# GpSimd takes seven low-weight subtractions of the long convolution's layer, and two output panels of the short convolutions run side by side

## The reference, cut to what matters

```python
def short_conv_mixer(h, w_in, conv_w, w_out):
    b_gate, c_gate, u = jnp.split(h @ w_in, 3, axis=-1)
    return (b_gate * depthwise_conv3(c_gate * u, conv_w)) @ w_out

def hyena_mixer(h, w_in, short_w, short_b, f_w1, ..., w_out):
    v, x1, x2 = jnp.split(depthwise_conv3(h @ w_in, short_w, short_b), 3, axis=-1)
    h_freq = hyena_filters(...)      # decayed filters, divided by their sum, in frequency
    z = x1 * long_conv(v, 0)
    z = x2 * long_conv(z, 1)
    return z @ w_out
```

## Time and profile before

| | |
|---|---|
| median of three runs | 1741.15 us (1740.19 to 1745.28) |
| profiled execution, its own time | 1742.05 us |
| its span | 1740.2 us |
| TensorE, VectorE, ScalarE, GpSimd busy | 97%, 71%, 56%, 1% |
| mean granted TensorE clock | 0.99 of full speed |
| phase `in2` and its filters | about 603 to 712 us |

### The profile page before, as it was taken

The page is one execution under the profiler, slowest core; times in us unless marked ns, Lnnn a source line. Parts: engine busy times, 40 slices in busy tenths (PEclk is TensorE's granted clock), DMA queues, the critical chain, the costliest instruction groups (busy, mean ns, idle before and its releaser), DMA issues.

```text
span 1740.2 us, 37287 instructions
## 1 busy us (share of the span) xinstructions
PE 1686.8 (97%) x13776; PEld 1594.9 (92%) x13776; DVE 1229.4 (71%) x2013; ACT 970.9 (56%) x1352; POOL 13.0 (1%) x20
## 2 busy tenths in 40 slices
PE   7999999999999999999999999999999999999997
PEld 7999999888999987569999999999999876799997
DVE  6887766587776687888776688776666665587764
ACT  4477744365775444206775446775455645477742
POOL 0000200000000000000000000000000000000000
PEclk9999999999999998999999999999999999999999
DMA  6577665433867554205666556667554432166662
GB/s 214 163 215 236 193 227 154 146 110 116 246 201 226 161 158 135 70 1 166 197 195 218 161 175 187 203 192 251 163 173 146 137 142 61 61 185 199 191 226 68
DMA packets 79547, 290.17 MB, mean 167 GB/s; under 512 B 9739, under 2 KB 12140, under 8 KB 79340
## 3 DMA queue, kind: packets, MB, share of 16 engines
q1 hardware_dynamic: 79468, 289.11, 53.1%
HBM read 288.03 MB, written 1.05 MB: 166 GB/s over the span
## 4 chain that ended last, share of the span: by engine, by line
PE 87%; DVE 9%; issue 2%; ACT 2%; DVEq 0%; DMA 0%; SPq 0%; ACTq 0%
PE bank L581 24%; PE bank L583 24%; PE bank L582 24%; DVE wlo L1553 2%; PE bank L869 2%; PE bank L856 1%; PE bank L810 1%; DVE conv_cv L1669 1%; PE bank L600 1%; PE bank L601 1%; PE bank L602 1%; PE bank L985 1%; DVE hy_z L1810 1%; PE bank L1081 1%; PE bank L1091 1%
## 5 line engine op out<-in xcount | busy, mean ns | idle before, releaser
L1185 ACT CAST whi<-raw 128x1024 fp32r<-128x1024 f32 (+1 forms) x490 | 539.2, 1102 | 330.0 <-PE bank L583 300.1
L581 PE MATMUL bank<-xq_h,whi 128*128 128x256 f32 x2384 | 664.1, 279 | 3.7 <-DVE wlo L1553 3.4
L583 PE MATMUL bank<-xq_l,whi 128*128 128x256 f32 x2384 | 657.7, 276 | 0.0
L582 PE MATMUL bank<-xq_h,wlo 128*128 128x256 f32 x2384 | 657.7, 276 | 0.0
L1553 DVE TENSOR_TENSOR wlo<-raw,whi 128x1024 fp32r<-128x1024 f32 (+1 forms) x491 | 629.9, 1283 | 6.3 <-ACT whi L1185 3.6
L581 PEld LDWEIGHTS bank<-xq_h,whi 128*128 128x128 f32 x2384 | 448.2, 188 | 14.1 <-issue 8.1
L582 PEld LDWEIGHTS bank<-xq_h,wlo 128*128 128x128 f32 x2384 | 448.1, 188 | 1.7 <-issue 1.7
L583 PEld LDWEIGHTS bank<-xq_l,whi 128*128 128x128 f32 x2384 | 448.0, 188 | 0.0
L583 PE MATMUL bank<-ffn_hl,whi 128*128 128x256 f32 x880 | 242.5, 276 | 0.0
L582 PE MATMUL bank<-ffn_hh,wlo 128*128 128x256 f32 x880 | 242.5, 276 | 0.0
L581 PE MATMUL bank<-ffn_hh,whi 128*128 128x256 f32 x880 | 242.4, 275 | 0.0
(11 more groups left out here) (342 smaller groups left out, 2379.7 us busy)
## 6 DMA issues: line engine op xcount, KB each, us to landing
raw<-in_w SPq DMA_DIRECT2D x414, 512.0 KB, 3.6
raw<-in_w SPq DMA_DIRECT2D x80, 704.0 KB, 4.1
att_bias<-in_bias SPq DMA_DIRECT2D x4, 512.0 KB, 5.5
hy_w<-in_filt_w SPq DMA_DIRECT2D x8, 256.0 KB, 5.5
hy_decay<-in_decay SPq DMA_DIRECT2D x4, 512.0 KB, 4.6
mla_uq<-in_uq SPq DMA_DIRECT2D x1, 1152.0 KB, 5.3
x<-in_xT SPq DMA_DIRECT2D x1, 1024.0 KB, 5.8
out<-x SPq DMA_DIRECT2D x8, 128.0 KB, 2.0
```

The costliest lines, as they stand in the source:

```text
L581: pe.matmul(ps, whi[:, slot, wc], hi[:, k, cols], start=first, stop=False)
L582: pe.matmul(ps, wlo[:, slot, wc], hi[:, k, cols], start=False, stop=False)
L583: mm = pe.matmul(ps, whi[:, slot, wc], lo[:, k, cols], start=False, stop=last)
L1185: nc.scalar.copy(slices(whi, p % RING, k, to), raw_slices(p % RING, k, to)).then_inc(panel_hi, 1)
```

## The change

GpSimd gets seven subtractions of phase `in2`: at steps 5, 8, 11, 14, 16, 19 and 22 VectorE leaves out `split_lo`. GpSimd waits for ScalarE's cast of that panel and subtracts. VectorE, after its two taps of the same step, waits for GpSimd's count and writes one element of a small tile, which raises `panel_lo` in its place, so that this semaphore is still raised by one engine and in order.

`merged` becomes `paired` with the phase's name, rows and semaphore as arguments. It is now called also for `out0` and `out3`, in place of `product`: two panels side by side over the eight slices, then six in turn.

```diff
+GPSIMD_SPLITS = (5, 8, 11, 14, 16, 19, 22)
-    eps = sb("eps", [P, 2])
+    eps = sb("eps", [P, 3])
+    gpsimd_lo = sem("gpsimd_lo")
...
-        def merged():
-
-            ph = PH["w_o"]
+        def paired(name, hi, lo, ready):
+
+            ph = PH[name]
             for j in range(2):
                 pe.wait_ge(panel_lo, ph.p0 + j + 1)
                 pe.wait_ge(bank_free, ph.t0 + j + 1)
             for k in range(K8):
-                pe.wait_ge(y_lo, YBASE["mrg"] + k + 1)
+                pe.wait_ge(ready[0], ready[1] + k + 1)
                 for j in range(2):
...
             for j in range(2, 8):
-                panel(ph, j // 4, j % 4, mg["yh2"], mg["yl2"], Q, None)
+                panel(ph, j // 4, j % 4, hi, lo, Q, None)
...
             if kind == "conv":
-                product(f"out{layer}", bufs["yh"], bufs["yl"], Q, (y_lo, YBASE[f"in{layer}"]))
+                paired(f"out{layer}", bufs["yh"], bufs["yl"], (y_lo, YBASE[f"in{layer}"]))
...
         mask_bias()
+        for step in GPSIMD_SPLITS:
+            p = PH["in2"].p0 + step + 3
+            pool.wait_ge(panel_hi, p + 1)
+            nc.gpsimd.tensor_tensor(wlo[:, p % RING, 0:K8 * P], raw[:, p % RING, 0:K8 * P],
+                                    whi[:, p % RING, 0:K8 * P].bitcast(F32), ALU.subtract).then_inc(gpsimd_lo, 1)
...
-                split_lo(ph, 0, i, j, k)
+                if i * 4 + j not in GPSIMD_SPLITS:
+                    split_lo(ph, 0, i, j, k)
 
                 dve.wait_ge(first_tap, TAPS["in2"] + j + 1 + 4 * i)
                 for t in (1, 2):
...
+                if i * 4 + j in GPSIMD_SPLITS:
+                    dve.wait_ge(gpsimd_lo, GPSIMD_SPLITS.index(i * 4 + j) + 1)
+                    V.memset(eps[0:1, 2:3], 0.0).then_inc(panel_lo, 1)
```

More of the change, by code:

```diff
@@ L920, in merged @@
                     wc = slice(k * P, (k + 1) * P)
-                    pe.matmul(ps, whi[:, slot, wc], mg["yh2"][:, k, Q], start=k == 0, stop=False)
-                    pe.matmul(ps, wlo[:, slot, wc], mg["yh2"][:, k, Q], start=False, stop=False)
-                    mm = pe.matmul(ps, whi[:, slot, wc], mg["yl2"][:, k, Q], start=False, stop=k == K8 - 1)
+                    pe.matmul(ps, whi[:, slot, wc], hi[:, k, Q], start=k == 0, stop=False)
+                    pe.matmul(ps, wlo[:, slot, wc], hi[:, k, Q], start=False, stop=False)
+                    mm = pe.matmul(ps, whi[:, slot, wc], lo[:, k, Q], start=False, stop=k == K8 - 1)
                     if k == K8 - 1:
@@ L1131, in _ @@
         product("mla_out", ml["yh"], ml["yl"], Q, None)
-        merged()
+        paired("w_o", mg["yh2"], mg["yl2"], (y_lo, YBASE["mrg"]))
         product("up4", *xs[norm], (x_lo, C * norm), norm)
```

## The result

The changed kernel takes 1749.65 us in the median of eight runs (1748.53 to 1751.46), the kernel before 1741.11 us in eight; the ratio is 1.0052, with an interval of 1.0043 to 1.0061. It is slower by 7.5 to 10.6 us. The forecast was 1749.1.

A forecast was written before the change was run, and what follows sets the result against it. TensorE bounds the kernel, busy 97%, with about 9 us of waits winnable. Holds 7.8, memsets +0.4, step 5 -0.3, side-by-side panels -0.2 make +8.0 us on 1741.15: 1749.1, range 1739.5 to 1752.0.

The forecast's parts named there:

- likeliest case: Long convolution's input product: GpSimd's reading holds VectorE's two-input operations; 1749.1 us, own range 1746.0 to 1752.0, chance 0.57.
- added elements: VectorE's seven added waits and one-element memsets, 0.1 us each; 0.4 us on the path at steps 5, 11, 14 and 19.
- second part: First two short-convolution output panels side by side: layer 3 trades a 0.67 us wait for 0.44, net -0.2; layer 0 nothing.
- The floor: VectorE's taps in the input product need ScalarE's first tap, so removing seven subtractions wins only 0.3 us of path.
- GpSimd's duration: Each 128x1024 subtraction on GpSimd taken as 2.4 us, between estimates of 2.2 and 2.7.
- The direction of the hold: A reading GpSimd operation was assumed to hold VectorE's two-input operations for its whole duration; the trace showed only GpSimd held.
- Step 5's hold: VectorE's subtraction due at 621.60 starts 1.7 us late behind GpSimd; taps and decayed filter come 1.25 us later.
- step 8's: VectorE's maximum of L1829, which TensorE waits for, is held until GpSimd stops reading at 635.6: +1.6 us.
- step 16's: VectorE's taps due at 669.29 wait for GpSimd until 671.15, straight before the maximum TensorE needs: +1.85 us.
- A: Rival: VectorE is not held, as GpSimd yields or both run; -0.1 us, 1741.0 us; chance 0.30.
- B: Rival: VectorE always wins and GpSimd is late, twice or so on the path; +1 us, 1742 us; chance 0.07.
- C: Rival: ScalarE's tap is not the floor, and TensorE's waits at L801 and L823 shrink; up to -6 us, 1735; chance 0.06.

The follow-up runs named there:

- experiment 3: The change without side-by-side output panels, its seven subtractions left out on both engines, VectorE's waits and one-element writes kept; 1739.0 us, ratio 0.9995.
- Experiment 8: Kernel before, with ScalarE's first tap put ahead of its cast in the long convolution's input product; 1738.32 us beside 1741.09, ratio 0.9984.
- experiment 5: The change without side-by-side output panels, with a GpSimd memset of the low weights in place of each subtraction; 1740.94 us in one run.
- experiment 6: The change without side-by-side output panels, with a one-input GpSimd copy in place of each subtraction; 1740.02 us in one run.
- experiment 7: Kernel before, with two subtractions (steps 6 and 15) moved to GpSimd, started just before VectorE's decayed-filter products; 1741.34 us in one run.
- experiment 10: Kernel before, with ScalarE's first tap ahead of its cast and seven subtractions left out on both engines, VectorE writing one element; 1738.08 us in one run.
- experiment 2: The changed kernel with no subtraction on GpSimd, only the first two output panels side by side; 1739.90 us beside 1740.45, ratio 1.0001.

## Why the prediction was right

Measured +8.5 us in the medians, forecast +8.0, in the middle of the likeliest case's own range. The mechanism is the one forecast. That the number came so near is in part luck: for the stretch the sum had 7.8 us of holds and 0.4 of added elements, and TensorE's waits there rose by 7.2, so with the 0.2 of the second part the waits account for 7.0 of the 8.5. The rest is not in TensorE's waits. In the profiled runs, 8.2 us apart, 0.8 of it is the clock and the start of the program, and 0.4 is left; in the others it is open.

- **What bounds the kernel.** That only about 9 us of TensorE's waits can be won there, and that the subtractions are on none of the long ones, held: experiment 3 took them away and changed the waits by 0.1.
- **The floor.** ScalarE's tap after the cast was named as what the taps wait for. After the change seven pairs of taps wait for it, idle 0.67 us each. Experiment 8 put it ahead of the cast, and the waits fell by 1.5 us.
- **GpSimd's duration.** Taken as 2.4, between 2.2 and 2.7 from three rows; measured 2.34 alone. The estimate from VectorE's ratio (2.2) was nearer than that from GpSimd's memset (2.7).
- **The direction of the hold.** This was the main assumption: the trace of before showed a held GpSimd and no held VectorE. The seven long operations and experiments 5, 6 and 7 show it, for GpSimd operations that read SBUF and VectorE operations with two SBUF inputs. The rule of the Trainium skill (SBUF — State Buffer, "Who interferes with whom") says this; the trace agrees, with 3.00 us for 1.22, and with nothing held beside a memset (1216 ns).
- **The prices.** Step 5's hold was put at 1.7 and is 1.78; step 8's at 1.6 and is 1.49; step 16's at 1.85 and is 1.68. By place of TensorE's waits: before the filter sums +5.2, and 0.3 more for late low weights, where steps 5, 8, 14 and 16 summed to 5.8; `wing_weights` +0.7 for 0.75; the first turn +0.5 for 0.8; the second turn +0.5 for 0.45. Sum 7.2 for 7.8. That low weights would once be late (0.3 us, behind step 5) was not foreseen.
- **The added elements.** 0.06 us each as taken from the earlier trace rows; the 0.4 charged to the path looks too much, since experiment 3 shows 0.1 less waiting with relief and writes together, where 0.3 won and 0.4 lost had been forecast.
- **The second part.** -0.2 by the exchange of 0.67 for 0.48, which the rows show and the times can't.
- **The rivals.** A is wrong on the hold. What it would have given stands in experiments 3 and 5: waits of 9.7 and 9.8 us for 9.8, and a ratio of 0.9995 in experiment 3. B falls, as VectorE lost 12.5 us. C falls with experiment 3; with the tap first it would have held for 1.1 us (experiment 10).

## What to carry to other kernels

An elementwise operation given to GpSimd is no relief of VectorE if it reads SBUF while VectorE has two-input operations to do: it took 2.34 us where VectorE had spent 1.13, and each one held VectorE for 1.5 to 2.05. Beside products with one input in PSUM it held nothing, and TensorE's waits rose by 0.2 us. A hold doesn't show as idle or as a wait of VectorE, only as an operation that takes longer than its like, so look there. And before an engine is relieved, look at what its next operation waits for; here it was the order of two operations on another engine.

## What the hardware showed that I had not expected

TensorE's granted clock in one and the same stretch was 0.91 of full speed in one kernel's run and 0.95 in another's with the same code there and the same waits (before and experiment 2), which is 2.6 us of length, more than most of these edits are worth. In before's trace it is half speed (1.2 GHz) for a time that begins 1.3 us after the first of the two waits before the filter sums has ended (635.3 us), and for another that begins within the second (668.7 to 672.3 us); in the rest of the stretch it is full speed (2.4 GHz). Window, length, busy time and count as above, then the granted clock:

```profile
636.70:643.30 6.60, 6.60 (x14) 3.50 (x15) 5.70 (x10) 3.19 (x6) 0.00 (x0) 0.50 0.55 172
643.50:670.60 27.10, 24.75 (x200) 22.64 (x199) 20.76 (x35) 12.43 (x16) 0.00 (x0) 1.00 0.56 166
670.80:680.90 10.10, 8.56 (x23) 5.60 (x23) 6.15 (x10) 2.72 (x4) 0.00 (x0) 0.50 0.34 109
681.10:710.40 29.30, 25.51 (x171) 20.79 (x169) 23.95 (x40) 10.44 (x14) 0.00 (x0) 1.00 0.18 54
```

What chose the longer or the shorter time at half speed was not settled.

GpSimd's durations in these profiles for 128 partitions of 32-bit values, where VectorE held nothing: two inputs 1.27 us for 512 columns and 2.34 for 1024, one input 1.04 for 1024, a memset 0.96. At 1024 columns the two-input one costs more than twice the others.
